# A split-precision GEMM kernel on one NeuronCore: the three split terms as the outer loop of a unit, and a later wait for the weights' low half

## The reference

```
first block, twice:   h += 0.5 * swiglu(rms(h), w_gu, w_down)
                      c_q, c_kv, k_pe, hq, hf, hi, hg, ga, gb = rms(h) @ w_in
                      y_a = mla(c_q, c_kv, k_pe) @ w_proj_attn ; y_b = hgrn2(hq, hf, hi, hg) @ w_proj_rec
                      h += (sigmoid(ga) * y_a + sigmoid(gb) * y_b) @ w_out
                      h += 0.5 * swiglu(rms(h), w_gu, w_down)
second block, once:   u, q, k, v, qi, ki, wi, gates = rms(x) @ w_in_2
                      y_ssm = s5(u) ; y_att = attention over the 128 keys per query that an index score selects
                      x += (sigmoid(g1) * y_ssm @ w_proj_ssm + sigmoid(g2) * y_att @ w_proj_attn) @ w_out_2
                      x += (silu(rms(x) @ w_gate) * (rms(x) @ w_up)) @ w_down
```

## Time and profile before

| what | value |
|---|---|
| median of 3 runs | 3546.17 us (3544.8 to 3550.06) |
| span of the profiled execution, first to last instruction | 3537.5 us |
| TensorE matmul busy | 3370.4 us (95%), 26596 matmuls |
| weight loads busy (overlap matmuls) | 3269.3 us (92%) |
| VectorE, ScalarE, GpSimd busy | 40%, 30%, 36% |
| mean granted TensorE clock | 0.968 |

### The profile page before, as it was taken

One profiled execution on the slowest core, in us unless ns is written; L12 is line 12 of the kernel. 1 busy time (PEld: TensorE's weight loads), 2 busy tenths in 40 slices (PEclk: granted clock), 3 DMA queues, 4 the chain that ended last, 5 costly groups with the idle time before them and its releaser, 6 DMA issues.

```text
span 3537.5 us, 66820 instructions
## 1 busy us (share of the span) xinstructions
PE 3370.4 (95%) x26596; PEld 3269.3 (92%) x26596; DVE 1414.9 (40%) x2183; ACT 1066.3 (30%) x1502; POOL 1280.5 (36%) x589
## 2 busy tenths in 40 slices
PE   7999989899999999999989899999998978999999
PEld 7999988798999999999988798999997866799999
DVE  4121343477521123121343487521127697452212
ACT  3222333222332223222333222332234324343222
POOL 3444432122443434444432122443443460144443
PEclk9999989999999999999989999999999997899999
DMA  3333221133333323333221133333323422133333
GB/s 121 90 91 91 84 63 49 40 91 107 96 89 89 90 86 88 89 89 89 82 63 49 40 93 108 98 89 89 89 86 99 104 60 93 33 101 91 94 95 95
DMA packets 544884, 299.47 MB, mean 85 GB/s; under 512 B 23280, under 2 KB 528624, under 8 KB 544560
## 3 DMA queue, kind: packets, MB, share of 16 engines
q1 hardware_dynamic: 514128, 258.77, 25.8%
q10 hardware_dynamic: 30560, 37.99, 3.3%
HBM read 278.49 MB, written 17.04 MB: 84 GB/s over the span
## 4 chain that ended last, share of the span: by engine, by line
issue 60%; POOL 22%; PE 13%; DVE 4%; POOLq 1%; ACTq 0%; ACT 0%; DVEq 0%
POOL wl L417 22%; PE pair L511 13%; POOLq L416 1%; DVE tmp L1629 1%; POOLq L421 0%; DVE negt L1708 0%; DVE top L1707 0%; DVE negt L1698 0%; ACTq L1156 0%; DVE tmp L1615 0%; PE aux L837 0%; DVE tmp L1627 0%; ACTq L1191 0%; DVE tmp L1758 0%; DVE tmp L1756 0%
## 5 line engine op out<-in xcount | busy, mean ns | idle before, releaser
L417 POOL TENSOR_TENSOR wl<-raw,wh 128x1024 fp32r<-128x1024 f32 (+4 forms) x549 | 1220.7, 2226 | 2238.5 <-ACT wh L880 2231.2
L511 PE MATMUL pair<-xh,wh 128*128 128x264 f32 (+1 forms) x5200 | 1074.5, 288 | 31.3 <-POOL wl L417 18.6
L511 PE MATMUL pair<-xl,wh 128*128 128x264 f32 (+1 forms) x5200 | 1061.8, 286 | 0.0
L511 PE MATMUL pair<-xh,wl 128*128 128x264 f32 (+1 forms) x5200 | 1060.6, 286 | 0.0
L511 PEld LDWEIGHTS pair<-xh,wh 128*128 128x128 f32 x5200 | 815.7, 191 | 42.0 <-issue 24.6
L511 PEld LDWEIGHTS pair<-xl,wh 128*128 128x128 f32 x5200 | 812.8, 190 | 0.0
L511 PEld LDWEIGHTS pair<-xh,wl 128*128 128x128 f32 x5200 | 811.2, 190 | 0.0
L880 ACT ACTIVATE wh<-raw 128x1024 fp32r<-128x1024 f32 (+4 forms) x549 | 527.6, 963 | 451.7 <-DMA raw<-ffn_w_down 160.2
L511 PE MATMUL pair<-ah,wh 128*128 128x264 f32 (+1 forms) x2312 | 477.0, 288 | 21.3 <-DVE gat L1253 6.1
L1253 DVE TENSOR_TENSOR tmp<-pair,rstd 128x528 f32<-128x528 f32 (+1 forms) x222 | 156.2, 704 | 843.0 <-PE pair L511 841.3
L511 PE MATMUL pair<-al,wh 128*128 128x264 f32 (+1 forms) x2312 | 472.1, 286 | 0.0
(11 more groups left out here) (282 smaller groups left out, 2814.9 us busy)
## 6 DMA issues: line engine op xcount, KB each, us to landing
raw<-ffn_w_gu SPq DMA_DIRECT2D x176, 512.0 KB, 3.8
raw<-w_in SPq DMA_DIRECT2D x103, 512.0 KB, 3.9
raw<-ffn_w_down SPq DMA_DIRECT2D x64, 512.0 KB, 3.7
raw<-ffn_w_down SPq DMA_DIRECT2D x32, 384.0 KB, 3.2
raw<-w_out SPq DMA_DIRECT2D x24, 512.0 KB, 3.7
raw<-w_ffn_gate SPq DMA_DIRECT2D x22, 512.0 KB, 3.8
raw<-w_ffn_up SPq DMA_DIRECT2D x22, 512.0 KB, 3.8
gate_scratch<-gst ACTq DMA_DIRECT2D x32, 264.0 KB, 2.8
```

The lines of the kernel that those rows point to most:

```text
L417: nc.gpsimd.tensor_tensor(wl[:, k % SPL, 0:n], raw[:, k % SPL, 0:n], wh[:, k % SPL, 0:n].bitcast(F32), ALU.subtract).then_inc(S["split_don ...
L511: mm = nc.tensor.matmul(pp[:, h, 0:th], w[:, s, kk * P:(kk + 1) * P], x[:, kk, t0 + h * th:t0 + (h + 1) * th], start=(kk == 0 and n == 0), ...
```

## The change

In `gemm` the wait at the start is for `split_hi` in place of `split_done`. The wait for `split_done` stands before the first matmul of the third term (the one that reads `wl`). Units without `ready` run all k-tiles of the first term, then all of the second, then all of the third. Units with `ready` keep the k-tile loop outside and the terms inside, with the new wait in k-tile 0. The matmuls, their number and the addresses that they read and write are the same. No other engine's program is changed.

```diff
-                pe.wait_ge(S["split_done"], U(l, k, i) + 1)
+                pe.wait_ge(S["split_hi"], U(l, k, i) + 1)
                 pe.wait_ge(S["evacuated"], U(l, k, i) + 1)
                 s = k % SPL
                 pp = pair[k % PAIRS]
-                for kk in range(kt):
-                    if ready is not None:
+                terms = ((wh, xs[0]), (wh, xs[1]), (wl, xs[0]))
+
+                def term(kk, n):
+                    w, x = terms[n]
+                    if n == 2 and kk == 0:
+                        pe.wait_ge(S["split_done"], U(l, k, i) + 1)
+                    for h in range(2):
+                        mm = nc.tensor.matmul(pp[:, h, 0:th], w[:, s, kk * P:(kk + 1) * P],
+                                              x[:, kk, t0 + h * th:t0 + (h + 1) * th],
+                                              start=(kk == 0 and n == 0), stop=(kk == kt - 1 and n == 2))
+                    return mm
+
+                if ready is None:
+                    for n in range(3):
+                        for kk in range(kt):
+                            mm = term(kk, n)
+                else:
+                    for kk in range(kt):
                         pe.wait_ge(*ready(kk))
-                    if sums is not None and kk == kt - 1:
-                        norm_sum(*sums)
-                    for n, (w, x) in enumerate(((wh, xs[0]), (wh, xs[1]), (wl, xs[0]))):
-                        for h in range(2):
-                            mm = nc.tensor.matmul(pp[:, h, 0:th], w[:, s, kk * P:(kk + 1) * P],
-                                                  x[:, kk, t0 + h * th:t0 + (h + 1) * th],
-                                                  start=(kk == 0 and n == 0), stop=(kk == kt - 1 and n == 2))
+                        if sums is not None and kk == kt - 1:
+                            norm_sum(*sums)
+                        for n in range(3):
+                            mm = term(kk, n)
                 mm.then_inc(S["gemm_done"], 1)
```

## The result

The changed kernel takes 3522.36 us in the median of 4 runs (3517.85 to 3529.87), against 3545.49 for the kernel before on the same chip. The ratio is 0.9943, 95% interval 0.9931 to 0.9956, so some 20 us went. The forecast was 5.8 us off and 3540.4 us, with 3534 as the low end of its range. The profiled execution took 3523.81 us.

The account below looks back on a forecast made before the run. It took PE's dense matmul stream to bound the kernel, gains coming only where PE stands still: 4.7 us in w_in_2 plus 1.1 at w_out, 5.8 us off the 3546.2 us median, 3540.4 us; own range 3537 to 3544, 8-in-10 range 3534 to 3556.

Parts of the forecast that it names:

- (f): The 542 units that didn't wait: one more semaphore wait each, and the new order of operands; both valued 0.
- The order of operands costs: Rival: weights and moving tile both change more often, a third of a nanosecond per matmul, 3549 us; chance 0.10.
- (a): Tenth unit of w_in_2: 2.2 us idle before it goes, plus 0.6 us from a shorter low clock; 2.8 us.
- (b): Twelfth unit of w_in_2: PE starts right after the norm2 sum, not on the low half; 1.6 us.
- (c): Thirteenth unit of w_in_2: the 0.3 us hole before it goes.
- (d): First units of the three w_out projections: four matmuls run ahead, the last `ml` limits the gain; 1.1 us.
- (e): First unit of the program: starts on the low half, but k-tile 2 waits for `xl` anyway; nothing gained.
- the rival of the broken run-ahead: Rival: a mid-unit wait holds up weight loads in each of 549 units, 3555 to 3595 us; chance 0.12.
- the FFN windows: Sign to check: two FFN windows show 820 and 857 matmuls in 100 us again; fewer would prove a slower rival.

Follow-up runs that it names:

- e1: The changed kernel with the low-half wait put back to the unit's start, so only the term order is new; 3529.39 us, ratio to before 0.9966.
- d2: Changed kernel's order with weights, moving operand or both held on k-tile 0 by stage, other products left out; 3514.28 us in one profiled execution.
- d6: New order, k-tile 0 of the moving operand read throughout, its start shifted from unit to unit, other products left out; 3516.80 us in one profiled execution.
- after: The changed kernel itself, with late wait and new order, against the kernel before; 3522.36 us, ratio 0.9943.
- e5: The kernel before with the late wait and new order in block 2's input projection (w_in_2) alone; 3534.67 us, ratio 0.9973.
- e2: The changed kernel with the old order in every unit, so only the waits are new; 3543.51 us, ratio to before 0.9999.
- e3: The changed kernel with the old order in block 2's 256-column stages except the input projection, late waits kept; 3513.63 us, ratio to before 0.9928.
- e4: Changed kernel with order chosen per stage: new at 264 columns, old at 256, others for w_in_2 and units that wait for operands; 3513.25 us, ratio to before 0.9915.
- d4: New order with the moving operand fixed on k-tile 1, 2 or 3 by stage, other products left out; 3531.39 us in one profiled execution.
- d1: The changed kernel with different loop orders by stage, such as PSUM bank outermost in the first and last FFN; 3527.62 us in one profiled execution.
- e6: e4 with the last FFN's and second w_out's operands packed at stride 2048 bytes, new order there; 3515.69 us, ratio to before 0.9931; profiled again 3505.96 and 3515.08 us.

## Why the prediction was wrong

**The step that failed is (f), "The new order of operands ... Value 0".** It is worth 12 us in e1, with the other sign than the rival I made of it ("The order of operands costs"). I had the size of the risk in the text, "half a nanosecond on 23,688 matmuls is 12 us either way", and then let the range end at 3534: its own bound, 3546.2 - 5.8 - 12, would have put it at 3528. The reading behind the value was at fault too. I took the earlier trace rows as "122 and 117 ns through every mix", and they are averages over one order; they could say nothing of another. The steps that differ "by 3 ns up or down without a rule" pointed to something beside the columns. What the runs put in place of the 0: -1.4 ns on the steps of the FFNs with 264 columns, some -16 us over four of them, and +1.8 ns on the last one, +6.0 us. That their net, 12 us, is just the 12 us of my half a nanosecond is chance: it is a difference of two larger terms. The order changes the sequence of places at which the moving operand is read, and d2 to d6 show that the place matters; why a place has its step is open.

**(a), the tenth unit: 2.8 forecast, 4.9 measured in after, 3.4 in e5.** From the ninth unit's start to the tenth's it is 9.50 us for 12.42, 2.9 less, against 2.2 for the hole. The hole behind the sum went as told (2.4 with the first matmul's slow start), and the pause before the sum is 2.28 us for 2.88, which I hadn't booked. In e1, with the old wait, it is 2.32, so that part comes with the order. The clock was mis-sized: I expected half of the fall of the earlier trace rows to stay; it didn't fall, and the unit took 2.0 us less (8.24 to 6.21). e5, where it did fall, gives 0.5 us for the same term, close to the 0.6 forecast. Right mechanism, a hole priced too low, and a clock term that chance decides.

**(b) 1.6, measured 1.95; (c) 0.3, measured -0.1.** The chain of evacuation, norm2 and high half moved with the tenth unit, as argued. Units of w_in_2 themselves became slower, 5.72 us for 5.61, which takes (c) away. (a) to (c): 4.7 forecast, 6.2 in after, 4.7 in e5.

**(d) 0.38 + 0.42 + 0.28.** After against e1, which differ only in the wait, over output projections and w_out: 0.26, 0.27 and 0.10 us, 0.6 for 1.1. PE took its two pairs ahead, but gave more back than the 0.1 booked in layer 0: the last `ml` moved no further forward, as forecast. The `ml` beside POOL's low halves took 2.90 us again (897.10 in the timeline of after, 2.88 in the earlier trace rows), against 0.69 alone (894.92). The rule of the Trainium skill, "SBUF — State Buffer", section on who interferes with whom, is that a VectorE operation with two SBUF inputs and a GpSimd operation that reads SBUF exclude each other; the trace agrees. (The 0.71 us that I called "in the open", at 903.49, lies for its last 0.49 us beside POOL's operation of 903.71.)

**(e) 0**, measured 0.07. **(f), the waits: 0**, right by e2; with it the rival of the broken run-ahead (3555 to 3595) is out.

**The sum.** Between e1 and after the later wait and the clock give 6.9 us in w_in_2 and 0.6 at w_out; the timed ratios (0.9966 and 0.9943, intervals that just touch) give 8. That is more than the 5.8 forecast, and 1.5 of it is the clock. The order gives 12 net. Of "what would show it" the FFN windows were the decisive line. Fewer matmuls in one was to prove a slower rival; one window had fewer, the other more, and the kernel was faster, which none of my cases had.

## What to carry to other kernels

When an edit reorders a dense stream of matmuls, price the order as a term of its own, with both signs, from the columns and the number of matmuls, and don't take an average over the old order as proof that order is free. Test orders stage by stage: here the same reordering gains 1.4 ns a matmul at 264 columns and loses 1.8 at 256, in this layout, and taking each where it pays (e3, e4) gave 3513 us against 3522 (ratios to before 0.9928 and 0.9915 against 0.9943, e4's interval just clear of the change's). Where a variant's runs lie in two groups, look at the rate of its densest stretch in several profiled executions before you believe either.

## What was not expected of the hardware

- At granted clock 1.00 (2.4 GHz) and with a weight load for every matmul, a 256-column matmul was followed by the next after 113.33, 117.8 or 120.0 ns in flat runs (113.33 x 2.4 is 272 cycles, 120.0 is 288), and a 264-column one after 120.0 to 126.7 ns. The Trainium skill, "TensorE: Matmul & The Clock Gate", section "Back-to-back issue gap", gives N/2.4 + 2.5 as the isolated gap, and says that in a stream both instructions of a pair set it. By that formula it would be, an estimate, 109 ns for 256 columns and 112.5 for 264. The measurement is above the formula throughout, and it varies at one N, which the page doesn't tell of.
- The step depends on where in SBUF the moving operand is read. With one start for all reads it follows the start modulo 256 bytes: at 256 columns from 113.3 ns at 64 to 120.0 at 128, the same values in three stages (d6). At some starts there are two or three steps, in one execution (d4, d6). It doesn't depend on which k-tile the weights come from (d2), and the number of weight changes doesn't order it (d1).
- The same program settles into 113.33 ns in one execution and 117.78 in another, for a whole stage of 68 units (e6). What sets the rhythm is open: I can't say what is being shared. The obvious candidate, something periodic in how the operand is fetched, is only argued.
- The clock fell after a pause of 2.30 us in e5 and not after 2.28 us in after: 1.5 us between two executions of the same code around it. Over all kernels with the late wait there, pauses of 2.20 to 2.87 us left it up seven times, and pauses of 2.11 to 3.75 us were followed by a fall eight times (e2 apart).
